# A diffusion trunk step: the second norm computed on token rows, with router logits taken in parts between the output products

## What is computed

```python
x = x + g1 * ((ga * y_a + gb * y_b + gc * y_c) @ lp['w_out'])
h2 = rms_norm(x, lp['rms2_g']) * (1 + sc2) + sh2
x = x + g2 * expert_choice_ffn(h2, lp['w_router'], lp['w1'], lp['w3'], lp['w2'])

def expert_choice_ffn(h, w_router, w1, w3, w2):
    cap = CAPACITY_FACTOR * L // N_EXPERTS
    aff = softmax(einsum('bld,de->ble', h, w_router), axis=-1)
    gate, idx = lax.top_k(swapaxes(aff, 1, 2), cap)
    xs = h[idx]                       # the rows that each expert chose
    hid = silu(xs @ w1) * (xs @ w3)
    ye = (hid @ w2) * gate[..., None]
    # the rows of ye are added back at idx
```

## Time and profile before

| what | us |
| --- | --- |
| median of three executions | 3169.63 |
| the profiled execution, whole | 3152.91 |
| its span, first to last instruction | 3151.1 |
| TensorE busy | 2894.2 (92%) |
| VectorE busy | 1954.8 (62%) |
| ScalarE busy | 1459.9 (46%) |
| GpSimd busy | 464.9 (15%) |
| granted clock of TensorE, mean over the span | 0.962 |

### The profile page before, as it was taken

One profiled execution on the slowest core, in us unless ns is written; L12 is line 12 of the kernel. 1 busy time (PEld: TensorE's weight loads), 2 busy tenths in 40 slices (PEclk: granted clock), 3 DMA queues, 4 the chain that ended last, 5 costly groups with the idle time before them and its releaser, 6 DMA issues.

```text
span 3151.1 us, 42363 instructions
## 1 busy us (share of the span) xinstructions
PE 2894.2 (92%) x16912; PEld 2243.4 (71%) x16912; DVE 1954.8 (62%) x1890; ACT 1459.9 (46%) x1594; POOL 464.9 (15%) x255
## 2 busy tenths in 40 slices
PE   5999989999985999999989999899999769999997
PEld 4888876888863666666579888678888546666664
DVE  2176664552335898888733866655433458889885
ACT  4135553112224777677542455421122436767774
POOL 0421110000001221222113311100000012222122
PEclk8999999999997999999989999999999979999998
DMA  6121143312217999999942211512212379999994
GB/s 252 61 69 48 48 146 129 101 54 67 80 54 262 331 380 375 368 370 372 382 138 65 61 48 61 206 39 100 76 56 70 122 255 367 376 366 375 374 370 155
DMA packets 238220, 601.08 MB, mean 191 GB/s; under 512 B 13376, under 2 KB 115936, under 8 KB 237312
## 3 DMA queue, kind: packets, MB, share of 16 engines
q1 hardware_dynamic: 225696, 552.87, 48.0%
q0 software_dynamic: 9312, 30.48, 3.9%
q10 hardware_dynamic: 3072, 15.73, 1.2%
HBM read 570.72 MB, written 28.31 MB: 190 GB/s over the span
## 4 chain that ended last, share of the span: by engine, by line
PE 83%; DVE 5%; ACT 4%; DMA 3%; issue 2%; PEld 1%; POOL 1%; SPq 1%; DVEq 0%; ACTq 0%; POOLq 0%; PEldq 0%
PE ps L1365 21%; PE ps L1366 20%; PE ps L1367 20%; PE ps L1403 8%; PE ps L1533 2%; PE ps L1509 2%; DMA xg<-h_dram,next_token 1%; PE ps L1522 1%; PE ps L1413 1%; DMA m_raw_b<-in_w_ada 1%; ACT probs L686 1%; PE ps L1859 1%; PE ps L1836 1%; PE ps L1802 1%; PE ps L1842 1%
## 5 line engine op out<-in xcount | busy, mean ns | idle before, releaser
L1280 DVE TENSOR_TENSOR m_lo<-m_raw_b,m_hi 128x2048 fp32r<-128x2048 f32 x192 | 439.4, 2289 | 72.9 <-ACT m_hi L861 70.6
L1280 DVE TENSOR_TENSOR m_lo<-m_raw_a,m_hi 128x2048 fp32r<-128x2048 f32 x192 | 438.8, 2288 | 70.4 <-ACT m_hi L861 67.9
L1365 PE MATMUL ps<-h_hi,w_hi 128*128 128x320 f32 x1408 | 454.3, 323 | 27.8 <-DVE h_lo L967 11.0
L861 ACT CAST m_hi<-m_raw_b 128x2048 fp32r<-128x2048 f32 x192 | 367.1, 1912 | 178.5 <-PE ps L1367 178.5
L1366 PE MATMUL ps<-h_lo,w_hi 128*128 128x320 f32 x1408 | 443.2, 315 | 0.0
L1367 PE MATMUL ps<-h_hi,w_lo 128*128 128x320 f32 x1408 | 443.1, 315 | 0.0
L861 ACT CAST m_hi<-m_raw_a 128x2048 fp32r<-128x2048 f32 x192 | 366.4, 1911 | 165.2 <-PE ps L1367 163.1
L1365 PE MATMUL ps<-m_hi,xs_hi 128*80 128x512 f32 x1024 | 409.0, 399 | 3.3 <-DVE xs_lo L1295 3.3
L1366 PE MATMUL ps<-m_lo,xs_hi 128*80 128x512 f32 x1024 | 406.4, 397 | 0.0
L1367 PE MATMUL ps<-m_hi,xs_lo 128*80 128x512 f32 x1024 | 404.5, 395 | 0.0
L528 ACT CAST w_hi<-raw 128x2048 fp32r<-128x2048 f32 x68 | 129.2, 1901 | 543.4 <-DMA raw<-in_w_gate 375.9
(11 more groups left out here) (268 smaller groups left out, 4705.4 us busy)
## 6 DMA issues: line engine op xcount, KB each, us to landing
m_raw_a<-in_w SPq DMA_DIRECT2D x192, 1024.0 KB, 7.3
m_raw_b<-in_w SPq DMA_DIRECT2D x192, 1024.0 KB, 7.4
raw<-in_w_in SPq DMA_DIRECT2D x72, 512.0 KB, 5.3
raw<-in_w_gate SPq DMA_DIRECT2D x48, 512.0 KB, 6.3
raw<-in_w_ada SPq DMA_DIRECT2D x32, 512.0 KB, 5.4
m_raw_a<-in_w_ada SPq DMA_DIRECT2D x8, 1024.0 KB, 12.0
m_raw_b<-in_w_ada SPq DMA_DIRECT2D x8, 1024.0 KB, 18.1
ada_raw_a<-in_w_ada SPq DMA_DIRECT2D x8, 1024.0 KB, 6.5
```

Source lines behind the costliest of these rows:

```text
L861: nc.scalar.copy(m_hi[:, n % RING], m_raw(slot)).then_inc(s["m_high"], 1)
L1280: nc.vector.tensor_tensor(m_lo[:, r], m_raw(slot), m_hi[:, r].bitcast(F32), ALU.subtract).then_inc(s["msplit"], 1)
L1365: pe.matmul(out, wh, xh, start=first, stop=False, skip_group_check=True)
```

## The change

The scale of the second norm commutes with the product by the router: with y = x * (gain * (1 + scale)), the logits are (y @ router) / root + shift @ router. The new code uses this and works on token rows:

- **Shift logits.** Between the two halves of gate product i = 9 TensorE computes shift @ router for both kinds of tokens (16 matmuls, semaphore `cst_ps`); VectorE copies them to `cst`. TensorE waits for this copy (`cst_out`) before the branch product of i = 9. The coefficients of the second norm move to i = 10.
- **Shift rows.** Before the first output product TensorE transposes the shifts, as broadcast columns, into rows (16 transposes into banks 4 to 7). ScalarE copies them to `shift_rows` (two copies) behind its eight `h_hi` casts and loads its root table there; the second output product waits for `shift_out`.
- **y and partial logits.** After each output product ScalarE writes y (four scaled copies) in place of two squares, and TensorE does `logit_part` of the tiles of one product earlier: 10 matmuls with 16 columns, behind products c = 1, 2, 3, and part 3 later.
- **Rows.** Once `x` is complete TensorE transposes `x` rows first and then y rows. VectorE copies the five x blocks out of PSUM; ScalarE squares each with its sum as a column (128 x 1 per block), and the root and reciprocal are 128 x 5. VectorE forms the five blocks of h2 straight from PSUM as y * (1/root) + shift row (`h2_row`), at three places between steps of the router.
- **Writes.** The rows leave by SyncE's queue, behind the first four loads of `m_raw_a`, and no longer by ScalarE's.
- **Slot numbers** count from 1 (the table `slot` too), so the subtraction of 1, and a memset of ones, are gone; the memset of `pos` stands earlier.
- **Gather.** GpSimd increments `gather_on` behind the instruction of the first gather, and VectorE waits for it before the four first low parts.

The diff, cut to its core:

```diff
@@ SyncE
                 chunks(0, 0, 0, False)
 
+                sp.wait_ge(s["xr_out"], TT * (l + 1))
+                sp.dma_start(out_lat.rearrange("(t p) d -> p t d", p=P), x_rows[:, 0:4]).then_inc(s["rows_out"], 16)
+                sp.dma_start(out_ctx, x_rows[:, 4]).then_inc(s["rows_out"], 16)
+                for t in range(TT):
+                    sp.wait_ge(s["h2_done"], TT * l + t + 1)
+                    sp.dma_start(h2_dram[t * P:(t + 1) * P], h2_rows[:, t]).then_inc(s["rows_out"], 16)
                 sp.wait_ge(s["rows_out"], seen("rows_out", 16 * (TT + 2)))
@@ GpSimd
                 gather()
+                pool.sem_inc(s["gather_on"], 1)
@@ ScalarE
+                act.wait_ge(s["shift_ps"], l + 1)
+                nc.scalar.copy(shift_rows[:, 0], flat[:, 6 * 512:6 * 512 + D])
+                nc.scalar.copy(shift_rows[:, 1], flat[:, 4 * 512:4 * 512 + D]).then_inc(s["shift_out"], 1)
+                nc.scalar.activation(st[:, 60:61], ones[:, 0:1], ACT.Sqrt)
...
-                    squares(2 * c, 2 * c + 2)
+                    for k in (2 * c, 2 * c + 1):
+                        for col, (a, b) in ((1, (0, LAT)), (0, (LAT, TOK))):
+                            ins = nc.scalar.activation(mm_[:, k, a:b], x[:, k, a:b], ACT.Copy, scale=coef[:, k, col:col + 1])
+                        ins.then_inc(s["y_done"], 1)
...
-                norm(24)
+                for t in range(TT):
+                    act.wait_ge(s["xr_out"], TT * l + t + 1)
+                    nc.scalar.activation(h2_rows[:, t], x_rows[:, t], ACT.Square, accum_out=st[:, 8 + t:9 + t]).then_inc(s["xr_sq"], 1)
+                act.wait_ge(s["xr_var"], l + 1)
+                nc.scalar.activation(st[:, 18:23], st[:, 13:18], ACT.Sqrt).then_inc(s["xr_root"], 1)
@@ VectorE
-                coefficients(32, "rms2")
-                norm()
...
+                for t in range(TT):
+                    dve.wait_ge(s["rows_ps"], 2 * TT * l + t + 1)
+                    b = 4 * (t % 2)
+                    nc.vector.tensor_copy(x_rows[:, t], flat[:, b * 512:b * 512 + D]).then_inc(s["xr_out"], 1)
...
+                def h2_row(t):
+
+                    dve.wait_ge(s["rows_ps"], 2 * TT * l + TT + t + 1)
+                    b = 4 * ((TT + t) % 2)
+                    nc.vector.scalar_tensor_tensor(h2_rows[:, t], flat[:, b * 512:b * 512 + D], st[:, 23 + t:24 + t], shift_rows[:, t // 4],
+                                                   ALU.mult, ALU.add).then_inc(s["h2_done"], 1)
...
                 choose(0)
                 slots()
+                dve.wait_ge(s["gather_on"], l + 1)
                 for n in range(RING):
                     low(0, n)
@@ TensorE
+                def logit_part(c):
+
+                    at = 328 + TT * EXPERTS * (c // 2)
+                    pe.wait_ge(s["y_done"], KT * l + 2 * c + 2)
+                    for t in range(TT):
+                        for k in (2 * c, 2 * c + 1):
+                            ins = pe.matmul(ps[:, 3 + 4 * (c % 2), at + EXPERTS * t:at + EXPERTS * (t + 1)], mm_[:, k, t * P:(t + 1) * P],
+                                            small_at("router")[:, k * EXPERTS:(k + 1) * EXPERTS], start=(k % 2 == 0), stop=(k % 2 == 1))
+                    return ins
...
+                    if c:
+                        logit_part(c - 1)
                 pe.sem_inc(s["d_done"], 1)
...
+                rows_of(0)
+                rows_of(1)
+                logit_part(3).then_inc(s["logits"], 1)
+                for i in range(2, 2 * TT):
+                    if i < TT + 2:
+                        pe.wait_ge(s["xr_out"], TT * l + i - 1)
+                    else:
+                        pe.wait_ge(s["h2_done"], TT * l + i - TT - 1)
+                    rows_of(i)
...
```

More of the change, by code:

```diff
@@ L575, in first_h @@
                         between()
-            def squares(a, b):
-                for k in range(a, b):
-                    nc.scalar.activation(mm_[:, k], x[:, k], ACT.Square).then_inc(s["sq"], 1)
-            def norm(shift):
-                act.wait_ge(s["row_a"], seen("row_a"))
-                nc.scalar.activation(row[:], row[:], ACT.Sqrt).then_inc(s["row_b"], 1)
-                act.wait_ge(s["mods_ready"], seen("mods_ready"))
-                for k in range(KT):
-                    act.wait_ge(s["tnorm"], seen("tnorm"))
-                    for c, (a, b) in ((1, (0, LAT)), (0, (LAT, TOK))):
-                        ins = nc.scalar.activation(mm_[:, k, a:b], mm_[:, k, a:b], ACT.Identity,
-                                                   scale=coef[:, k, c:c + 1], bias=mods[:, shift + k, c:c + 1])
-                    ins.then_inc(s["hnorm"], 1)
             act.wait_ge(s["const_in"], 80)
@@ L920, in split_low @@
                 dve.sem_inc(s[f"raw_free{rslot}"], 1)
-            def norm():
-                dve.wait_ge(s["ss"], seen("ss"))
-                nc.vector.tensor_scalar(row[:].rearrange("p (a n) -> p a n", a=2), ps[:, 0:2, 0:HALF], 1.0 / D, EPS,
-                                        ALU.mult, ALU.add).then_inc(s["row_a"], 1)
-                dve.wait_ge(s["row_b"], seen("row_b"))
-                link(nc.vector.reciprocal(row[:], row[:]))
-                for k in range(KT):
-                    nc.vector.tensor_tensor(mm_[:, k], x[:, k], row[:], ALU.mult).then_inc(s["tnorm"], 1)
             def coefficients(scale, g):
@@ L1226, in _ @@
[L1226 removed]
+                link(nc.vector.memset(pos[:], -1.0))
+                for t in range(TT):
+                    dve.wait_ge(s["rows_ps"], 2 * TT * l + t + 1)
+                    b = 4 * (t % 2)
+                    nc.vector.tensor_copy(x_rows[:, t], flat[:, b * 512:b * 512 + D]).then_inc(s["xr_out"], 1)
+                dve.wait_ge(s["logits"], l + 1)
@@ L1447, in fold_ada @@
                 ins.then_inc(s["ada_t"], 1)
-            def sum_squares(n_in, sem_in):
-                for k in range(n_in):
-                    pe.wait_ge(s[sem_in], seen(sem_in))
-                    for c, (a, b) in enumerate(halves):
-                        ins = pe.matmul(ps[:, c, 0:HALF], ones[:], mm_[:, k, a:b], start=(k == 0), stop=(k == n_in - 1), skip_group_check=True)
-                ins.then_inc(s["ss"], 1)
             def tile(c, t):
@@ L1750, in between @@
                             ln_sums(4, lambda g: (zc[:, g, 0:LAT], zc[:, g, LAT + CPAD:CRUN]), None)
+                        if i == 9 and (j, c) == (1, 0):
+                            wait_set(1)
+                            for h in (1, 0):
+                                for k in range(KT):
+                                    ins = pe.matmul(ps[:, 4, EXPERTS * (1 - h):EXPERTS * (2 - h)], mods[:, 24 + k, h:h + 1].to_broadcast([P, P]),
+                                                    small_at("router")[:, k * EXPERTS:(k + 1) * EXPERTS], start=(k == 0), stop=(k == KT - 1))
+                            ins.then_inc(s["cst_ps"], 1)
                         if i == 7 and (j, c) == (1, 0):
@@ L1777, in _ @@
                 pe.sem_inc(s["split_free1"], 1)
+                wait_set(1)
+                for h, b in ((1, 6), (0, 4)):
+                    for k in range(KT):
+                        ins = pe.transpose(flat[:, b * 512 + k * P:b * 512 + (k + 1) * P], mods[:, 24 + k, h:h + 1].to_broadcast([P, P]), ident[:])
+                ins.then_inc(s["shift_ps"], 1)
+                def logit_part(c):
[6 more added lines that the diff above has]
+                    return ins
                 for c in range(4):
@@ L1795, in _ @@
                 pe.wait_ge(s["g2_cols"], seen("g2_cols"))
                 for k in range(KT):
-                    ins = pe.transpose(flat[0:SLOTS, 6 * 512 + k * P:6 * 512 + (k + 1) * P], g2_cols[:, k, :], ident[:])
+                    ins = pe.transpose(flat[0:SLOTS, 2 * 512 + k * P:2 * 512 + (k + 1) * P], g2_cols[:, k, :], ident[:])
                 ins.then_inc(s["g2_ps"], 1)
-                for k in range(KT):
-                    pe.wait_ge(s["hnorm"], seen("hnorm"))
-                    for c, (a, b) in enumerate(halves):
-                        ins = pe.matmul(ps[0:EXPERTS, 4 + c, 0:HALF], small_at("router")[:, k * EXPERTS:(k + 1) * EXPERTS], mm_[:, k, a:b],
-                                        start=(k == 0), stop=(k == KT - 1), skip_group_check=True)
```

128 lines of the change are left out of this document (61 added, 67 removed).

## The result

| | before | after |
| --- | --- | --- |
| median, us (executions) | 3162.34 (6) | 3139.57 (6) |
| spread, us | 3156.12 to 3169.69 | 3132.52 to 3142.74 |
| profiled execution, us | 3152.91 | 3132.52 |
| its span, us | 3151.1 | 3130.7 |
| TensorE busy in the span, us | 2894.2 | 2885.2 |

The ratio after to before is 0.9923, 95% interval 0.9904 to 0.9943: faster by 0.77%, about 24 us (the two medians differ by 22.8). The forecast was 3125 in a range of 3105 to 3150, from a sum of -36.5 us against the profiled execution; the profiles differ by 20.4.

What follows compares the result with a forecast made beforehand. TensorE is busy nearly everywhere, and the waits from last output product to first expert matmul are on the path. Layers of -19.7 and -16.8 sum to -36.5 us; 3125 was put between 3116.4 and 3133.1, range 3105 to 3150.

Steps and rivals of the forecast that it cites:

- rows in DRAM long before they are needed: Writes of the h2 rows: all over near 26 us after the last output product, 22 us ahead of need.
- low parts next in line: Before the first expert matmul: VectorE's 8.88 us of low parts, no longer the gathered data, would be what is late.
- 16 shift-logit matmuls: In the merge, where TensorE is full: 0.15 us each, so 2.4 us added a layer.
- partial logits 0 and 1: Between the output products: 20 matmuls on TensorE's path, 3.0 us added a layer, 6.0 at half clock.
- gap filled, warmer start: Shift transposes in TensorE's 5.06 us gap may keep 2.4 GHz for the next product: 1 us gained, ends 0 and 2.
- T to first `max`: End of last output product (T) to first max: T + 22.4 instead of T + 37.1 and T + 34.4, -14.7 and -12.0.
- choice of tokens: First max to the end of next_token: a memset and the subtraction of 1 go, -1.1 us a layer.
- S to E: End of next_token (S) to first expert matmul (E): S + 11.7 instead of S + 20.0 and S + 19.8, -8.3 and -8.1.
- The additions ahead of T: TensorE's added work before the last output product ends: +4.4 us a layer, ends +3.4 and +8.4.
- stays blocked: Rival at the first gather: gather_on fires at hand-over, VectorE still blocks descriptors; 16.4 us lost, -20.1 left; chance 0.32.
- late rows: Slower case: rows landing later than about T + 67 in both layers turn the result into a loss; chance 0.03.
- time is given back in the experts: Rival in the first expert: weight loads collide with the second gather, 4 us a layer lost, -28.5 left; chance 0.08.

Runs made afterwards that it cites:

- e2: Changed kernel with gather_on raised by a small GpSimd memset behind the gather instead of the queue's own increment; ratio to the kernel before 0.9919.
- e1: Changed kernel without VectorE's wait on gather_on, so it goes from next_token straight to the first low part; ratio to the kernel before 0.9973.
- e5: Changed kernel with the 16 shift-logit matmuls moved from product i = 9 into TensorE's idle stretch ahead of the first output product; ratio to before 0.9910.
- e7: Changed kernel with the five h2 blocks scaled by ScalarE and their shift rows added by GpSimd, instead of VectorE; ratio to the kernel before 0.9893.
- e8: Changed kernel with gather_on raised by a GpSimd memset behind the gather, and xs_lo behind the second low part, not the fourth; ratio to before 0.9906.
- e9: Changed kernel with the edits of e5, e7 and e8 together; 3115.67 us, ratio to the kernel before 0.9853.
- e6: Changed kernel with partial logits 0, 1 and 2 computed behind the last output product instead of between the products; ratio to the kernel before 0.9968.

## Why the prediction was right, and where its sizes were off

Three mechanisms were right: a shorter way from T to the choice, a gather held up less by VectorE, rows in DRAM long before they are needed. The fourth, low parts next in line, was not: in the changed kernel they end at 980.10, and `xs_lo` then waits 2.46 us for the gathered data; only e2 shows the order that I had described. The sum was too large by 16.1 us of 36.5. That the time lies within the range is owed to the width of the range, which reached down to a gain of 20 us, and not to the sum. By its own steps, both layers together:

| step | forecast | measured | missed |
| --- | --- | --- | --- |
| 16 shift-logit matmuls | 4.8 | 7.1 | 2.3 |
| partial logits 0 and 1 | 6.0 | 8.3 | 2.3 |
| gap filled, warmer start | -2.0 | -3.5 | -1.5 |
| a fall of the clock | none | 3.1 | 3.1 |
| T to first `max` | -26.7 | -25.0 | 1.7 |
| choice of tokens | -2.2 | -1.9 | 0.3 |
| S to E | -16.4 | -14.3 | 2.1 |
| elsewhere | 0 | 5.8 | 5.8 |
| sum | -36.5 | -20.4 | 16.1 |

- *The additions ahead of T.* This is a reading that was wrong. I took the row "x8, 1.2 us" of the earlier trace rows for eight matmuls of 0.15 us. It was four, each recorded twice, so 0.30, and the new ones take 0.23 and 0.24. The loop in the code (two matmuls at L1446 for this operand in each of two layers) against the count of records would have shown it, and so would against the code: the 16 matmuls with ones stand there as x32, and I called them 32. The updates of `x` in the second layer stand 14.62, 16.70 and 16.69 us apart where all were 14.62: 2.07 for each part.
- *The clock.* I priced a gain at the gap and no loss behind the new small matmuls. In the first layer the last product took 18.25 us instead of 16.69 (window 906 to 910 above), in the second the fall came at 2469 behind part 2 and made the 16 transposes of the first two x blocks 3.56 us instead of 1.95. A window of it:

```profile
2471.00:2473.00 2.00, 2.00 (x12) 2.00 (x11) 1.22 (x1) 0.57 (x3) 0.00 (x0) 0.50 1.03 416
```

  Without it T to `max` would be 23.3 in both layers; in the table it stands in the row of its own. In the changed kernel and e1, e2, e5, e7, e8 and e9 thirteen of the fourteen layers have such a fall during or behind one of the groups; the second layer of e5 has none. M to `max` is 186.3 to 186.6 in four kernels (after, e1, e2, e8) and both layers, wherever in it the fall lies. The 37.1 us from T to `max` that I started from held such a fall too (10.52 instead of 8.89 us for the matmuls with ones), which is part of why the second layer had 34.4. What decides where the clock falls was not tested and stays open.
- *T to `max`.* T + 22.4 was forecast, T + 23.3 came. Copies took 1.22 (1.25), h2 blocks 1.28 (1.27), the squares 1.06 and 0.19. What I had not seen: VectorE waits 0.95 and 0.35 us for transposes between h2 blocks. The exponential's table load (1.28 us) ended just as its input was ready.
- *The gather.* The rival "stays blocked" had the right event and only part of its consequence: the increment does fire at the hand-over, but one low part got in front and not four. The row that I cited for a start without harm, 0.44 us behind the gather's start in the steady state, did not carry over to 0.17 us ahead of it. S to E is 12.7 us in the mean instead of 11.7. The Trainium skill (SBUF — State Buffer, Who interferes with whom) infers that operations with two inputs in SBUF leave descriptor making alone. For the instruction as a whole e1 against the changed kernel shows otherwise, with 8.78 against 2.99 us; since it also reads its indices from SBUF, the runs do not say whether that reading or the making of descriptors was held up.
- *Choice.* The scan with a broadcast column of ones takes 1.21 us as before; pricing it at nothing was right.
- *Elsewhere.* The same code ran 3.5 us longer up to M, 3.6 longer from E to the second layer's M, and 1.3 shorter at the end. The eleven profiled executions spread over 755.7 to 762.6 for the first and 1318.6 to 1326.1 for the second, and the kernel before holds the lowest of each. So its profile was a favourable draw, as the prediction suspected when it put the median 16.7 us above it; by the ratio the gain is 24 us, and the profiles' 20 understate it.
- *The sums.* The prediction's ends were added up wrongly: its own terms make -45 and -17, not -48 and -16. Its limit for late rows, T + 67, is that of the first layer; in the second it is T + 64. Neither changes the forecast.
- *Rivals.* By the time alone the blocked gather, priced at -20.1, would have fitted the profiles' -20.4 better than my -36.5; only the row of the gather, 2.99 us and not 8.78, tells them apart. That time is given back in the experts has no support and is not quite excluded: e8 starts 3.8 us sooner than e2 and takes as long from E to M (1323.5 and 1323.1 us), while the three kernels with a blocked gather took 1318.6, 1325.3 and 1319.0 and the eight others 1320.5 to 1326.1, a spread in which 2 us can hide. The rows were not late: the loads of `m_raw_b`, which wait for `rows_out`, were issued from 949.68 (T + 27.3, where I had T + 26), over 21 us ahead of the gather.

The experiments divide the gain: the wait 0.40%, all else 0.27%. I had put 16 us on the first and 20 on the second; 12.6 and 8.5 came, each give or take 5, so which of the two is the larger is not settled by the times. By the rows of the profiles S to E gives 14.3 us and the way up to S 11.9, of which the new small matmuls on a full TensorE take back 15.4.

## What to carry to other kernels

Count the matmuls in the code against the records in the trace before dividing: matmuls on plain fp32 operands stood there twice in this case. Do not judge rivals by the time alone: a wrong sum and a rival can meet at one number, and a row of the trace tells them apart. If an indirect DMA sits on the critical path, look at what VectorE does just then, and release VectorE by an instruction that the same GpSimd executes behind it, not by the queue's increment; in the traces this frees the gather, though in time e2 did not differ from the changed kernel beyond the intervals. Small matmuls are cheap only in TensorE's idle stretches, and even there a fall of the clock may come with them (e9, not e5); spread out, they did less harm than close together.

## What the hardware showed that I had not expected

- A low part that starts 0.17 us before the gather's record holds it up for 2.0 us (2.99 against 0.99), and then the gather gets in although the next low parts follow at once; with the low parts begun 0.96 us ahead it waits for all four (8.78). Why one start lets it in after the first and the other does not, no run here shows.
- The granted clock fell to 0.50 while TensorE was busy all the time: for about 3 us in the changed kernel (906 to 910), for 17 us in e6 (929 to 946), each time during or behind groups of fp32 matmuls with 16 columns. The same groups passed at 1.00 in the second layer of e5, and in the kernel before the fall at 914 to 917 came during matmuls with 320 columns, behind 2.27 us of idle time.
- GpSimd's additions of 128 x 1024 fp32 numbers in SBUF took 2.3 us each beside VectorE's `max` and `match_replace` on 16 partitions, which kept their 0.68 and 0.66 us.
